# Moving the two rings of split weights to other distances in SBUF in a two-layer decoder trunk

## The reference

```python
for layer in range(DEPTH):                      # DEPTH = 2
    i = layer // 2
    y = rmsnorm(h, norm_g[layer, 0])
    if layer % 2 == 0:
        y = even_mixer(y, even_w_in[i], even_w_out[i], cmp_pe[i], cmp_w1[i], cmp_w2[i])
    else:
        y = odd_mixer(y, odd_w_in[i], odd_w_out[i])
    h = h + rmsnorm(y, norm_g[layer, 1])
    y = conv_ffn(rmsnorm(h, norm_g[layer, 2]), ffn_w_up[layer], ffn_conv_w[layer],
                 ffn_conv_b[layer], ffn_w_down[layer])
    h = h + rmsnorm(y, norm_g[layer, 3])
```

## Time and profile before

| | |
|---|---|
| median of 3 runs | 657.37 us |
| span of the profiled execution | 655.8 us |
| TensorE matmuls busy | 646.6 us (99%), 3572 instructions |
| TensorE weight loads busy | 539.4 us (82%) |
| VectorE busy | 460.1 us (70%) |
| ScalarE busy | 385.1 us (59%) |
| GpSimd busy | 163.8 us (25%) |
| granted TensorE clock | 1.00 of full speed nearly throughout |
| DMA | 115.60 MB, mean 176 GB/s |

### The profile page before, as it was taken

How to read it: one execution, slowest core, us unless ns; L and a number is a source line. 1 busy time by engine, 2 the same in 40 slices (tenths; PEclk the granted TensorE clock), 3 DMA queues, 4 the chain that set the end, 5 groups by cost and what they waited for, 6 DMA issues and landing times.

```text
span 655.8 us, 9975 instructions
## 1 busy us (share of the span) xinstructions
PE 646.6 (99%) x3572; PEld 539.4 (82%) x3574; DVE 460.1 (70%) x627; ACT 385.1 (59%) x561; POOL 163.8 (25%) x123
## 2 busy tenths in 40 slices
PE   9999999999999999999999999999999999999996
PEld 6888887577888888888888888777888888888885
DVE  6498766877697878786457645676688788886532
ACT  7556355865757667666335535765567676767330
POOL 0323300001053444441001000680123434343000
PEclk9999999999999999999999999999999999999999
DMA  8987633004456363637652663304255554544601
GB/s 350 339 296 284 228 129 129 1 6 189 132 198 245 133 249 131 236 149 268 242 196 69 253 240 144 129 1 192 97 184 200 182 202 168 216 151 177 248 1 64
DMA packets 18971, 115.60 MB, mean 176 GB/s; under 512 B 2911, under 2 KB 3453, under 8 KB 6013
## 3 DMA queue, kind: packets, MB, share of 16 engines
q1 hardware_dynamic: 17789, 111.52, 45.7%
q10 hardware_dynamic: 1152, 3.67, 1.7%
HBM read 114.14 MB, written 1.05 MB: 176 GB/s over the span
## 4 chain that ended last, share of the span: by engine, by line
PE 93%; DVE 2%; POOL 2%; ACT 1%; issue 1%; DVEq 0%; POOLq 0%
PE ps L1423 27%; PE ps L1430 14%; PE ps L1380 11%; PE ps L1381 11%; PE ps L1382 11%; PE ps L1452 5%; PE ps L1507 2%; POOL sb_splo L1352 1%; PE ps L1751 1%; PE ps L1635 1%; PE ps L1371 1%; PE ps L1901 1%; PE ps L1679 1%; PE ps L1601 1%; PE ps L1738 1%
## 5 line engine op out<-in xcount | busy, mean ns | idle before, releaser
L778 DVE TENSOR_TENSOR wlo<-raw,whi 128x2048 fp32r<-128x2048 f32 x99 | 227.0, 2325 | 72.7 <-ACT whi L413 72.6
L413 ACT CAST whi<-raw 128x2048 fp32r<-128x2048 f32 x99 | 185.7, 1916 | 48.6 <-PE ps L1382 42.0
L1423 PE MATMUL ps<-xpair,whi 128*128 128x512 f32 x768 | 183.4, 391 | 0.0
L1423 PEld LDWEIGHTS ps<-xpair,whi 128*128 128x128 f32 x768 | 141.2, 188 | 27.6
L1430 PEld LDWEIGHTS ps<-xpair,wlo 128*128 128x128 f32 x768 | 98.5, 191 | 3.7
L1430 PE MATMUL ps<-xpair,wlo 128*128 128x256 f32 x768 | 99.6, 283 | 0.0
L1328 POOL TENSOR_TENSOR hidf<-act_g,conv 128x512 f32<-128x512 f32 x22 | 76.1, 3460 | 85.0 <-ACT act_g L671 85.0
L1380 PE MATMUL ps<-whi,hid_hi 128*128 128x512 f32 x176 | 68.5, 389 | 0.0
L1381 PE MATMUL ps<-wlo,hid_hi 128*128 128x512 f32 x176 | 68.5, 389 | 0.0
L1382 PE MATMUL ps<-whi,hid_lo 128*128 128x512 f32 x176 | 68.5, 389 | 0.0
L1380 PE MATMUL ps<-whi,xpair 128*128 128x512 f32 x168 | 67.7, 403 | 0.0
(11 more groups left out here) (197 smaller groups left out, 788.2 us busy)
## 6 DMA issues: line engine op xcount, KB each, us to landing
raw<-in_weights SPq DMA_DIRECT2D x101, 1024.0 KB, 5.0
c_gpost<-in_gpost ACTq DMA_DIRECT2D x4, 512.0 KB, 5.0
raw<-in_weights SPq DMA_DIRECT2D x3, 512.0 KB, 6.8
c_gpre<-in_gpre ACTq DMA_DIRECT2D x3, 512.0 KB, 4.3
h<-in_x SPq DMA_DIRECT2D x2, 512.0 KB, 3.8
out<-h SPq DMA_DIRECT2D x4, 256.0 KB, 2.0
raw<-in_weights SPq DMA_DIRECT2D x2, 256.0 KB, 4.8
t<-in_masks SPq DMA_DIRECT2D x1, 512.0 KB, 12.1
```

What stands on the lines that cost most here:

```text
L413: act.copy(whi[:, slot, :], raw[:, slot, :]).then_inc(hi_done, 1)
L778: dve.tensor_tensor(wlo[:, slot, :], raw[:, slot, :], whi[:, slot, :].bitcast(F32), ALU.subtract).then_inc(lo_done, 1)
L1423: pe.matmul(ps[:, b0 + m, :], whi[:, slot, cols], xpair[:, kt].rearrange("p a c -> p (a c)"), start=kt == 0, stop=kt == KT - 1, skip_group ...
```

## The change

Each slot of `whi` and of `wlo` is followed by 4 unused elements (16 bytes), a gap of 64 elements (256 bytes) stands between the two rings, and one of 32 elements (128 bytes) behind the second. In all that is 512 bytes in a partition, so that all that is declared after it lies where it lay modulo 512. Relative to the activations, the four high slots begin at 0, 16, 32 and 48 bytes, and the four low ones at 320, 336, 352 and 368, modulo 512. The views that the instructions use keep their shape. No instruction, wait or transfer is added, removed or put in another place; `raw` keeps its place.

```diff
+PITCH = 4
...
         raw = sb("raw", [P, RING, UNIT])
-        whi = sb("whi", [P, RING, UNIT], F32R)
-        wlo = sb("wlo", [P, RING, UNIT], F32R)
+        whi = sb("whi", [P, RING, UNIT + PITCH], F32R)[:, :, 0:UNIT]
+        sb("low_gap", [P, 64])
+        wlo = sb("wlo", [P, RING, UNIT + PITCH], F32R)[:, :, 0:UNIT]
+        sb("stage_gap", [P, 32])
```

## The result

The changed kernel takes 663.77 us (663.62 to 663.88, 4 runs), the kernel before, on the same chip, 657.41 us (657.18 to 657.55, 4 runs). The ratio is 1.0096, with a 95% interval of 1.0082 to 1.0110: slower by 6.4 us, and outside my range. The profiled execution spans 661.9 us against 655.8, so all of it is inside the span.

The account below looks back on a forecast made before the run. TensorE's matmul count times pitch was taken to bound the kernel. The change's terms all summed to 0: 655.8 us span + 0 + 1.6 to the median = 657.4 us; 8-in-10 range 650.5 to 661.0, no measurable change 0.46.

Parts of the forecast that it names:

- What bounds the kernel: Whole span: TensorE, busy 99%; number of matmuls times their pitch sets the time, 543.7 us of it touched by the change.
- The split steps: VectorE and ScalarE splitting weights, 2325 and 1916 ns a unit: unchanged and hidden by waiting, so 0 on the path.
- The load beside it costs a matmul of 512 columns about 1 ns at distance 0 ... I take 0.: 1992 wide matmuls: 388 ns without a load beside, 389 with one; at most 2.0 us to gain, taken as 0.
- The loads at 0, 64 and 320 lie within 5 ns of each other: Load durations of 186, 189 and 191 ns at other distances, read as evidence that distance hardly matters.
- the unit with every second token: Stationary operand read with an 8-byte step: matmuls 394 ns, pitch 231; as a cost 6.9 us for half the slots, taken as 0.
- Matmuls of 256 columns: 768 matmuls with wlo loaded: 283 against 277 ns may be a clash; bound 4.3 us gained, taken as 0.
- The first rival: Faster by the loads: clash beside wlo ends at 320 to 368, 4.3 us, 6.3 with wide matmuls, giving 651.1 us; chance 0.27.
- slower by the odd slots: Loads 16 or 48 bytes off cost matmuls 5 ns in half the slots: 6.9 us, giving 664.3 us; chance 0.22.
- The sign that I named for it: For the slower case: L1423's mean rises over 391 ns, with every second unit slower than its neighbours.
- Faster by far more: Place of the loaded operand could take 10 ns from each of 2760 matmuls: 27.6 us, giving 629.8 us; chance 0.05.
- the 10 ns between the two mask products: Two successive mask matmuls, 389 and 379 ns, with different loads beside them; read as kind of load, not place.
- The Trainium skill: Documentation: TensorE's two ports never wait, and 16-byte lines are crossed as often as before; by these rules place changes nothing.

Follow-up runs that it names:

- the low half alone: Kernel before with all four low slots at 320 bytes from the activations and the high slots at 0: 660.55 us, ratio 1.0051.
- the half-line run: Kernel before with xpair, both rings, hid_hi and hid_lo all 8 bytes on, every distance 0 modulo 256: 666.65 us.
- the half period: Kernel before with slots' (high, low) distances at (0, 256), (256, 256), (256, 0) and (0, 496) bytes: 657.9 us.

## Why the prediction was wrong

**What bounds the kernel** was right. TensorE's waits stay nothing: the longest is the one at the start, the same as in the earlier trace rows:

```profile
PE ps L1503 <- POOL c_mask L1267: 1.3, 1, 1.3
```

The number of matmuls times their pitch set the time, and a few ns on each decided.

**The split steps** were right: 2326 and 1915 ns, 0 on the path.

**"The load beside it costs a matmul of 512 columns about 1 ns at distance 0 ... I take 0."** This is the step that failed. It holds two errors. First, a measurement at distance 0 bounds what can be gained there, but not what another distance can cost; 0 was the good case. The term was 1992 matmuls x 0; it came to 2.7 us in the group of L1423 (now L1426) and 4.4 in the token-form groups and L1455 and L1510 together, 7.1 us. Second, the test itself measured something else. The matmul that ends the same stage in the changed kernel, again with no load beside it, in the groups at 414.45 us:

```profile
L1385 PE MATMUL ps<-whi,xpair 128*128 128x512 f32 x1 | 0.4, 397 | 0.0
```

388 ns in the earlier trace rows, 397 here, without any load recorded during it. It is 388 also where all these operands moved by 32 bytes, and 397 with the low half alone at 320, where this product moves `whi` at distance 0 and only the one before it moves `wlo`. So "no load beside it" did not mean "free of the effect of places": the record of a matmul changes with the place of an operand that only its neighbour uses. The single matmul without a load could not tell the load's share.

**"The loads at 0, 64 and 320 lie within 5 ns of each other"**, my evidence against both signs, was no evidence. The loads keep 188 ns in the steady stretch while the matmuls go from 389 to 394. The only row that spoke was the one I set aside: the unit with every second token, 394 ns and 231 ns of pitch, which is what the changed token form now shows everywhere. That the cause is the same in both isn't shown.

**Matmuls of 256 columns.** I took 0 of a bound of 4.3 us; 0.8 came. The first rival's gain is there, in the low half alone it is 1.2 us (99.6 to 98.4), so it gives a fifth to a good quarter of the bound: 16 in 1.89 us, where I named 1.81. The most that any kernel showed is 3.5 us (96.1) and 1.84, with the low parts of both sides moved by 64 and `xpair` laid out anew. That what ends there is a clash of the load with `xhi` isn't shown.

**The rival "slower by the odd slots"**, at 0.22, was right in sign and, with 664.3 us, near in size, but not in where, so the size is partly luck. I had 5 ns in half of the slots in every form. It came as 5 ns in three of four slots of the channel form, and some 5 ns in all slots of the token form, the one with the high part at 0 too, since its low part stands at 320. The sign that I named for it, every second unit slower, didn't come: three of four did.

**"Faster by far more"** fell: no placement gave more than the 178 matmuls in the window, and the best row of 16, 3.63 us at 496 and 508 against 3.65, has 226.9 ns on average against 228.1. Where the 10 ns between the two mask products come from was not tested.

**The Trainium skill** (SBUF — State Buffer, "Who interferes with whom") gives TensorE two independent ports and no waiting. What I drew from it, that place can't matter, is wrong for these float32r products: the same instructions with the same granted clock and no longer waits go from 226.9 to 232.1 ns when an operand is moved by tens of bytes. Whether it is these two ports that disturb each other no run shows. Its lines of 16 bytes ("Specifications (TRN2)") would fit the half-line run, 666.65 us against 657.46, but not the fast row at 508; and with all starts at multiples of 16, as in the change itself, the time still rose.

**What stays open** is which two accesses clash. A clash of the load with the moving stream wherever their addresses are alike would make distance 0 the worst place, and it is among the best for the wide matmul; besides, the matmul without a load shows the effect. That neighbours carry it would fit the records, in which a matmul lasts 389 ns (its end is modelled) and the next begins after 227; but nothing here separates the streams of two neighbours from the loads between them. The places between 0 and 256 also differ among each other (3.73, 3.69, 3.67 us for 16) in a way that no theory of mine gives.

## What to carry to other kernels

Where TensorE is the bound by products like these (float32r, a load for each matmul), give all its large operands, loaded and moving, the same address modulo 256 bytes, at a multiple of 32 (0 and 32 were good, 8 was not), and look at the pitch (matmuls in a window, or 16 in the chain) and not at the durations of loads when a tensor is added or padded: innocent gaps ahead of one or both rings cost 0.4 to 1.3% here (660.28 to 665.8 us), except where they kept it at 0 modulo 256. A cost that reads as 1 ns in the present layout says nothing about another layout: before a term is set to 0, ask whether the present is the good case. And price an edit by the row that comes nearest to what it does to the access pattern, even if it is a slow oddity in a corner of the trace.

## What the runs showed of the hardware that I had not expected

- The pitch of a float32r matmul of 512 columns depends on the relative place of operands: in the down-projection 226.9 ns at 0 and 256 bytes, and 230.8 to 233.5 ns in the window of every kernel with its rings elsewhere (but for the half period, where one slot is off); single slots away from 0 have 228.7 to 240.0 ns. Where all operands move by 32 bytes together it doesn't change.
- The narrow matmul of the channel form mostly wants the opposite: 16 take 1.91 us at 0 and 256, 1.84 to 1.89 at most other places, and 1.90 to 1.92 at 128, 352, 368, 384, 500 and 508. Since its ring also serves the token form, no placement tried had the gain (1.2 us at 320) without the loss.
- A product is slowed by the place of an operand that only its neighbour uses: 394 ns for all three lines with `wlo` alone at 320. And a row of 16 wide matmuls with all its operands at 0 takes 3.65 to 3.70 us by the places of the narrow rows beside it.
- A start 8 bytes on, in the middle of a 16-byte line, costs some 9 us of 657.5 even with all distances 0 modulo 256 (one run, 666.65 us).
